# Two picks side by side: a pair of expert rows per visit of the value matmuls, with four PSUM banks

## The chip, the cores and the metric

The kernel runs on one core of a Trainium2 chip. The metric is the device time of one execution in microseconds; for the kernel before there are three runs and one profiled execution.

## What is computed

One layer of a hybrid decoder, in fp32, for a prompt of 1024 positions and 8 sequences of 4 new positions (1056 rows in all): an RMS norm and one input projection feed a convolution, an RWKV head group and stick-breaking attention; their outputs are mixed through one output projection. Then comes the part that the change touches, a product-key mixture of experts (PEER). For each row and each of 8 heads, 16 of 16384 experts are chosen; each expert is one row of a table u and one of a table v:

```python
q = (xb @ w_query).reshape(T, PEER_HEADS, 2, PEER_DK // 2)
s = jnp.einsum('thcd,hcnd->thcn', q, sub_keys)
s1, i1 = lax.top_k(s[:, :, 0], 16); s2, i2 = lax.top_k(s[:, :, 1], 16)
# the 16 x 16 sums, their 16 best (top_s) and the expert numbers e
gate = jax.nn.softmax(top_s, axis=-1)
act = jax.nn.gelu(jnp.einsum('thkd,td->thk', u_tab[e], xb))
return jnp.einsum('thk,thkd->td', (gate * act), v_tab[e])
```

The result is added to the row, and a last RMS norm gives the output.

## The kernel before

The first stages (`project`, `scan_rwkv`, `finish_rwkv`) end at about 990 us. All the rest is `peer`. It works on blocks of 128 rows (`NBLK` = 9, the last one with the 32 sample rows only) and on turns, one head of one block each (`PH` = 8 turns a block). A turn of a full block has 16 picks: for pick k, POOL gathers for each of the 128 rows its k-th expert, u and v rows together, 8 KB a row, into one of 8 slots of `uv` (`RING` = 8). In the last block the 32 rows share the 128 partitions in four groups, so a turn has 4 picks. Picks are taken in pairs (`GP` = 2), numbered m over the whole run.

The engines follow fixed orders written out by hand, with semaphores between them. For each pair:

- POOL (L1270) waits for `uv_free` to reach m - 7 and for the experts of the turn, and issues one gather for each pick.
- DVE (L1535) forms the dot product of u and the normed row, one pick at a time; in between it chooses the experts of the turn after the next (`choose`, L1293 to L1320) in four pieces, and `weigh` (L1342) multiplies gate and activation.
- ACT (L1686) computes the gelu, and (L1694) writes for each pick a diagonal matrix of the weights, `diag`, with a ring of four; each raises `diag_done` by one.
- PE (L1896; L1892 in the last block) multiplies the diagonal with the v half of the slot and accumulates into PSUM over all 128 picks of the block, then raises `uv_free`. It also makes the scores of a later turn (`score`, L1713) and, beside each pair, a piece of attention or output projection for the next block (`beside`).

When a block is complete, DVE adds PSUM to the residual rows `x1` (`add_values`, L1356, L1353). It does so in the next block after that block's first pair has been weighed; PE's first value matmul of the new block waits for it (`summed`). The 64 x 64 matmuls use a quarter of the array each: row half r of the partitions goes to bank `Y[r]`, and the column half j holds columns j*512 to j*512+511 of the output.

In an earlier stage of `peer`, 16 query blocks are folded with the keys into `wk`, with four PSUM banks in rotation (`WK`, L1081).

Of the kernel before, what the change touches and what calls it, by code (L numbers as in the profile page):

```python
# [11 lines left out]
ALU = mybir.AluOpType  # L12
# [4 lines left out]
D = 1024  # L17
# [3 lines left out]
NS = DB * DS  # L21
# [24 lines left out]
PH = 8  # L46
# [923 lines left out]
def peer(nc, io, sb):  # L970

    RING = 8
    GP = 2
# [9 lines left out]
    last = lambda b: b == NBLK - 1  # L983
# [4 lines left out]
    groups_of = lambda t: picks_of(t // PH) // GP  # L988
    after = lambda t: at_pick(t, picks_of(t // PH))
    rows = [slice(r * HT, (r + 1) * HT) for r in range(2)]  # L990
    SUMS = lambda b: 2 if last(b) else 4

    Z, LOGIT, SOFT, LATER, DIFF, OUT, KEEP = 0, 9, 10, 10, 12, 12, 21
    K_PAGES, V_PAGES = -4, 5
# [52 lines left out]
    with ExitStack() as ctx:  # L1047
# [3 lines left out]
        uv = t_("uv_rows", [P, RING, 2 * D])  # L1051
        h2, h2t, x1 = t_("p_h2", [P, 2, D]), t_("p_h2t", [P, DC, P]), t_("p_x1", [P, 2, D])
# [11 lines left out]
        diag = t_("diag", [P, 2 * GP, P])  # L1064
# [11 lines left out]
        zb, sa, sw = logit[:, 0, 0:NK * HQ], logit[:, 1, 0:NK * HQ], soft[:, 0, 0:NK * HQ]  # L1076
        suf = after_[:, :, :].rearrange("p h q -> p (h q)")[:, 0:NPG * HQ]
        ps = lambda name: ctx.enter_context(nc.psum_tensor(name, [P, 512], F32))
        Y = [ps(f"peer_y{r}") for r in range(2)]
        S, B = ps("peer_s"), [ps(f"beside{n}") for n in range(3)]  # L1080
        WK = [Y[0], Y[1], ps("wk_a"), ps("wk_b")]  # L1081
        const_in, close_in, key_in, wq_in = sem("p_const"), sem("p_close_in"), sem("p_key_in"), [sem(f"p_wq_in{n}") for n in range(2)]
        wk_done, wk_kept, eps_set = sem("wk_done"), sem("wk_kept"), sem("p_eps_set")
        uv_in = [sem(f"uv_in{n}") for n in range(RING)]
        dotted, uv_free = sem("dotted"), sem("uv_free")
        gelu_done, weights_done, diag_done = sem("gelu_done"), sem("weights_done"), sem("diag_done")
        score_done, score_kept, exps_done = sem("score_done"), sem("score_kept"), sem("exps_done")
        summed, y_ready, y_out = sem("p_summed"), sem("y_ready"), sem("y_out")
# [188 lines left out]
        def _(dve):  # L1277
# [67 lines left out]
            def add_values(b):  # L1345

                s = b % 2
                dve.wait_ge(uv_free, after(PH * b + PH - 1))
                dve.wait_ge(KV.sem, KV.at("x1", b))
                for k in range(2):  # L1350
                    half = slice(k * 512, (k + 1) * 512)
                    if last(b):
                        nc.vector.tensor_tensor(x1[0:NS, s, half], x1[0:NS, s, half], Y[k][0:NS, :], ALU.add).then_inc(summed, 1)  # L1353
                    else:
                        for r in range(2):
                            nc.vector.tensor_tensor(x1[rows[r], s, half], x1[rows[r], s, half], Y[r][rows[k], :], ALU.add).then_inc(summed, 1)  # L1356

            def normalise(b):

# [164 lines left out]
            for t in range(TURNS):  # L1524
                b, h = divmod(t, PH)
                if h == 0:
                    dve.wait_ge(KV.sem, KV.at("h2", b))
                for q in range(groups_of(t)):
                    g = at_group(t, q)
                    for k in range(GP):  # L1530
                        m = g * GP + k
# [16 lines left out]
                    if not last(b):  # L1548
                        beside(b, h * groups_of(t) + q)
            add_values(NBLK - 1)  # L1550
            normalise(NBLK - 1)

        @block.scalar
        def _(act):
# [9 lines left out]

            def norm(b):
                s, n = b % 2, rows_of(b)
                act.wait_ge(summed, 4 * b + SUMS(b))
                F.did(nc.scalar.activation(h2[0:n, b % 2, :], x1[0:n, s, :], ACT.Square, accum_out=ssq[0:n, 0:1]), "ssq")
                act.wait_ge(F.sem, F.at("ssq", b))
                F.did(nc.scalar.activation(rstd[0:n, :], ssq[0:n, 0:1], ACT.Sqrt, bias=sb.eps[0:n, 0:1], scale=1.0 / D), "root")  # L1570

            def close_root(b):

                act.wait_ge(KV.sem, KV.at("x1", b))
                KA.did(nc.scalar.activation(h2[:, b % 2, :], x1[:, b % 2, :], ACT.Square, accum_out=cssq[:, 0:1]), "ssq")
                act.wait_ge(KA.sem, KA.at("ssq", b))
                KA.did(nc.scalar.activation(crstd[:, :], cssq[:, 0:1], ACT.Sqrt, bias=sb.eps[:, 0:1], scale=1.0 / D), "root")
# [87 lines left out]
            for hc in range(2 * PH):  # L1665
                for j in range(2):
                    act.wait_ge(wk_done, 2 * hc + j + 1)
                    nc.scalar.activation(wk[:, 4 * j:4 * j + 4, hc * P:(hc + 1) * P], WK[(2 * hc + j) % 4][:, :], ACT.Copy).then_inc(wk_kept, 1)
            close_root(0)
# [7 lines left out]
            for t in range(TURNS):  # L1677
                b, h = divmod(t, PH)
                eye = ident4 if last(b) else ident
                n = rows_of(b)  # L1680
                for q in range(groups_of(t)):
# [8 lines left out]
                    for k in range(GP):  # L1690
                        m = g * GP + k
# [13 lines left out]
        def _(pe):  # L1705
            def score(t):
                b, h = divmod(t, PH)
                if h == 0:
                    pe.wait_ge(KA.sem, KA.at("t1", b))
                if t:  # L1710
                    pe.wait_ge(score_kept, t)
                for c in range(DC):
                    ins = nc.tensor.matmul(S[:, 0:HN], h2t[:, c, :], wk[:, c, h * HN:(h + 1) * HN],  # L1713
                                           start=c == 0, stop=c == DC - 1)
                ins.then_inc(score_done, 1)
# [135 lines left out]
            def beside(b, n):  # L1851

                beats(b, n, attend, sample)
                if n - CLOSE in range(DC):
                    close_y(b + 1, n - CLOSE)
                if n == TURN:
                    close_turn(b + 1)
# [5 lines left out]
            for hc in range(2 * PH):  # L1863
                g = hc // WQ
                pe.wait_ge(wq_in[g % 2], 16 * (g // 2 + 1))
                for j in range(2):
                    if hc >= 2:
                        pe.wait_ge(wk_kept, 2 * hc + j - 3)
                    for c in range(4):
                        ins = nc.tensor.matmul(WK[(2 * hc + j) % 4][:, c * P:(c + 1) * P], wq[g % 2][:, hc % WQ, (4 * j + c) * P:(4 * j + c + 1) * P],  # L1870
                                               keys[:, hc, :], start=True, stop=True)
# [9 lines left out]
            for t in range(TURNS):  # L1881
                b, h = divmod(t, PH)
                if h == 0 and b:
                    pe.wait_ge(summed, 4 * b)
                for q in range(groups_of(t)):
                    for k in range(GP):
                        m = at_group(t, q) * GP + k
                        begin, end = h == 0 and q == 0 and k == 0, h == PH - 1 and m + 1 == after(t)
                        pe.wait_ge(diag_done, m + 1)
                        if last(b):  # L1890
                            for j in range(2):
                                ins = nc.tensor.matmul(Y[j][0:NS, :], diag[:, m % (2 * GP), 0:NS],  # L1892
                                                       uv[:, m % RING, D + j * 512:D + (j + 1) * 512], start=begin, stop=end)
                        else:
                            for r, j in ((0, 0), (1, 0), (0, 1), (1, 1)):
                                ins = nc.tensor.matmul(Y[r][rows[j], :], diag[rows[r], m % (2 * GP), rows[r]],  # L1896
                                                       uv[rows[r], m % RING, D + j * 512:D + (j + 1) * 512], start=begin, stop=end)
                        ins.then_inc(uv_free, 1)
                    if q == (1 if groups_of(t) > 1 else 0) and t + LEAD + 1 < TURNS:
                        score(t + LEAD + 1)  # L1900
                    if not last(b):
                        beside(b, h * groups_of(t) + q)
# [158 lines left out]
```

## Time and profile before

| | |
|---|---|
| three runs | 4021.95, 4023.74, 4036.12 us (median 4023.74) |
| the profiled execution | 4021.95 us, of which its span is 4020.1 us |
| PE busy | 2858.3 us, 71% |
| DVE busy | 2654.0 us, 66% |
| ACT busy | 1485.8 us, 37% |
| POOL busy | 1368.1 us, 34% |
| moved by the transfers | 1248.22 MB, mean 310 GB/s |
| mean granted TensorE clock | 0.85 of full speed |

Busy time is summed over the whole span. The span begins with the first instruction and ends with the last; the profiled execution has 1.85 us outside it. An engine that is busy two thirds of the whole may be the limit in one stage and wait in another, so the stages are read one at a time. The DMA share is that of the core's 16 DMA engines, as a mean; it can come out slightly over 1.

### The profile page before, as it was taken

To read this page: it belongs to the slowest core of one execution; us is meant where nothing else is said; L and a number is where in the kernel's file an instruction comes from. 1 tells how busy PE (TensorE), PEld (TensorE's weight loads), DVE (VectorE), ACT (ScalarE), POOL (GpSimd) and SP (SyncE) were. 2 spreads that over 40 slices of the span, in tenths; PEclk is the share of its full clock that TensorE was granted. 3 is DMA by queue.
4 is the path that set the end of the run, shared out by engine and by line. 5 is a ranking of instruction groups with operands and counts; after the bars stand their busy time and mean duration, and the time that the engine had idled before them with its cause. 6 is when DMAs were issued, how large, how long until landed. Compare 5 with 4: busy or idle time off the path is not lost.

```text
span 4020.1 us, 53279 instructions
## 1 busy us (share of the span) xinstructions
PE 2858.3 (71%) x18798; PEld 1340.5 (33%) x18798; DVE 2654.0 (66%) x6645; ACT 1485.8 (37%) x3026; POOL 1368.1 (34%) x1230
## 2 busy tenths in 40 slices
PE   6999777736666676667767676777777766767656
PEld 3545566615222232223223232332323322232211
DVE  1376233342877777877877787678768776777776
ACT  1121222113426234532743483267338522332222
POOL 0000000000443544454354435334444545453421
PEclk8999999868888778878878887888789887788778
DMA  2101100015999999999999999999999999999964
GB/s 81 40 27 59 59 1 0 2 63 181 411 417 408 417 412 411 411 413 415 404 406 414 410 385 417 417 405 404 417 411 405 390 418 413 412 416 411 406 261 169
DMA packets 225745, 1248.22 MB, mean 310 GB/s; under 512 B 33200, under 2 KB 62032, under 8 KB 90224
## 3 DMA queue, kind: packets, MB, share of 16 engines
q0 software_dynamic: 160256, 1132.54, 69.1%
q1 hardware_dynamic: 65264, 112.87, 7.9%
q8 instruction: 118, 1.93, 0.2%
q14 instruction: 107, 0.88, 0.1%
HBM read 1232.20 MB, written 13.11 MB: 310 GB/s over the span
## 4 chain that ended last, share of the span: by engine, by line
DMA 34%; DVE 15%; PE 13%; ACT 7%; issue 5%; POOL 4%; SPq 0%; DVEq 0%; ACTq 0%; POOLq 0%
DMA uv_rows<-in_peer_uv,expert 28%; PE peer_y L1896 8%; DVE uv_rows L1535 5%; DMA pages_ring<-out_k_new 5%; POOL uv_rows L1270 3%; PE peer_s L1713 2%; ACT L1686 1%; ACT diag L1694 1%; ACT L1632 1%; PE peer_y L1892 1%; DVE same L1316 1%; DVE same L1314 1%; DVE pick L1318 1%; DVE weights L1342 1%; PE beside L1734 1%
## 5 line engine op out<-in xcount | busy, mean ns | idle before, releaser
L1896 PE MATMUL peer_y<-uv_rows,diag 64*64 64x512 f32 x8192 | 1285.7, 758 | 793.6 <-ACT diag L1694 772.7
L1270 POOL DMA_INDIRECT uv_rows<-in_peer_uv,expert x1056 | 1201.3, 1138 | 1712.4 <-PE peer_y L1896 1316.2
L1535 DVE CUSTOM_DVE_ANT_0 uv_rows<-uv_rows,p_h 128x1024 f32<-128x1024 f32 x1056 | 1276.5, 1225 | 512.7 <-DMA uv_rows<-in_peer_uv,expert 508.7
L1896 PEld LDWEIGHTS peer_y<-uv_rows,diag 64*64 64x64 f32 x8192 | 318.8, 160 | 1489.0 <-ACT diag L1694 1106.9
L1694 ACT ACTIVATE diag<-p_ident,weights 128x128 f32<-128x128 f32 x1024 | 355.2, 394 | 498.7 <-DVE weights L1342 496.3
L1686 ACT ACTIVATE gelu<-hidden 128x2 f32<-128x2 f32 x528 | 107.4, 203 | 1120.2 <-DVE hidden L1535 1116.1
L523 PE MATMUL proj<-mix,w_in_tile 128*128 128x512 f32 x672 | 298.0, 602 | 18.3 <-DVE mix L332 18.3
L1713 PE MATMUL peer_s<-wk,p_h2t 128*128 128x256 f32 x1152 | 280.1, 398 | 2.3 <-ACT p_h2t L1585 1.3
L1713 PEld LDWEIGHTS peer_s<-wk,p_h2t 128*128 128x128 f32 x1152 | 222.2, 198 | 107.6 <-issue 76.7
L1686 ACT ACT_TABLE_LOAD x196 | 251.5, 1283 | 3.5
L633 POOL COPY v_c<-prc 128x192 f32 (+1 forms) x17 | 5.8, 343 | 627.4 <-POOLq L86 347.5
L523 PEld LDWEIGHTS proj<-mix,w_in_tile 128*128 128x128 f32 x672 | 127.8, 193 | 172.2 <-issue 153.3
L1342 DVE TENSOR_TENSOR weights<-gelu,p_gate 128x2 f32<-128x2 f32 x528 | 85.1, 161 | 130.5 <-ACT gelu L1686 121.2
L1809 PE MATMUL beside<-q_padded,pages_ring 128*128 128x256 f32 x216 | 70.6, 448 | 81.4 <-DMA pages_ring<-out_k_new 80.6
L1892 PE MATMUL peer_y<-uv_rows,diag 128*32 128x512 f32 x128 | 80.9, 796 | 58.8 <-ACT diag L1694 52.8
L1734 PE MATMUL beside<-w_out_rows,mix_block 128*128 128x512 f32 x180 | 93.4, 645 | 22.6 <-DMA w_out_rows<-in_w_out 22.6
L348 DVE TENSOR_TENSOR prc<-prc 128x1088 f32<-128x1088 f32 x11 | 14.2, 1291 | 119.8 <-ACT prc L217 119.8
L1563 ACT ACT_TABLE_LOAD x71 | 91.1, 1283 | 1.3
L212 ACT ACTIVATE prc<-proj 128x512 f32<-128x512 f32 x15 | 9.0, 598 | 221.4 <-PE proj_tails L523 221.4
L1535 DVE DVE_READ_ACCUMULATOR2_ANT hidden<- 128x1 f32 x1056 | 87.5, 83 | 0.0
L1250 POOL DMA_INDIRECT pages_ring<-in_cache_k,page_rows x64 | 76.7, 1199 | 23.0 <-issue 18.9
L1809 PEld LDWEIGHTS beside<-q_padded,pages_ring 128*128 128x128 f32 x216 | 39.8, 208 | 133.1 <-issue 110.5
(324 smaller groups left out, 3935.6 us busy)
## 6 DMA issues: line engine op xcount, KB each, us to landing
w_out_rows<-in_w_out SPq DMA_DIRECT2D x72, 512.0 KB, 8.1
uv_rows<-in_peer_uv,expert POOLq DMA_INDIRECT x1056, 12.5
w_in_tile<-in_w_in SPq DMA_DIRECT2D x24, 512.0 KB, 3.8
uv_rows<-in_w_query SPq DMA_DIRECT2D x4, 2048.0 KB, 10.1
pages_ring<-out_k_new SPq DMA_DIRECT2D x36, 192.0 KB, 31.7
pages_ring<-out_v_new SPq DMA_DIRECT2D x36, 192.0 KB, 25.8
p_x<-in_x_rows SPq DMA_DIRECT2D x9, 512.0 KB, 8.0
mix<-in_xT SPq DMA_DIRECT2D x8, 528.0 KB, 6.8
```

The source lines that it names most:

```text
L523: last = nc.tensor.matmul(out, w[:, i % 3, c, :], h[:, c, lo:lo + size], start=c == 0, stop=c == DC - 1)
L1270: pool.indirect_dma_start(out=uv[:, m % RING, :], out_offset=None, in_=io["peer_uv"], in_offset=bass.IndirectOffsetOnAxis(ap=expert[:, t % ...
L1342: nc.vector.tensor_tensor(wgt[:, g % 2, :], gel[:, g % 2, :], gate[:, t % 4, q * GP:(q + 1) * GP], ALU.mult)\
L1535: nc.vector.tensor_tensor_reduce(out=uv[:, m % RING, 0:D], in0=uv[:, m % RING, 0:D], in1=h2[:, b % 2, :], scale=1.0, scalar=0.0, op0=ALU.m ...
L1563: nc.scalar.activation(expo[:, :], top[:, :], ACT.Exp, bias=neg[:, 0:1], accum_out=esum[:, 0:1]).then_inc(exps_done, 1)
L1686: nc.scalar.activation(gel[:, g % 2, :], hid[:, g % 2, :], ACT.Gelu_apprx_tanh).then_inc(gelu_done, 1)
L1694: nc.scalar.activation(diag[:, m % (2 * GP), 0:n], eye[:, 0:n], ACT.Copy, scale=wgt[:, g % 2, k:k + 1])\
L1713: ins = nc.tensor.matmul(S[:, 0:HN], h2t[:, c, :], wk[:, c, h * HN:(h + 1) * HN], start=c == 0, stop=c == DC - 1)
L1734: ins = nc.tensor.matmul(B[n][:, :], left[:, :], wo[:, c % 2, n * 512:(n + 1) * 512], start=c == 0, stop=c == DC - 1)
L1809: ins = nc.tensor.matmul(B[0][:, i * P:(i + 2) * P], page[:, kt % 4, h // 2 * P:(h // 2 + 1) * P], qpad[:, h:h + 2, :], start=True, stop=True)
L1892: ins = nc.tensor.matmul(Y[j][0:NS, :], diag[:, m % (2 * GP), 0:NS], uv[:, m % RING, D + j * 512:D + (j + 1) * 512], start=begin, stop=end)
L1896: ins = nc.tensor.matmul(Y[r][rows[j], :], diag[rows[r], m % (2 * GP), rows[r]], uv[rows[r], m % RING, D + j * 512:D + (j + 1) * 512], sta ...
```

## The change

The value matmuls visit the picks in pairs. PE waits for both diagonals of a pair (`diag_done` at m + 2), then makes the eight matmuls of a full block with the column half c of the array given to pick m + c, and the two halves of the columns one after the other, each in a bank of its own. So there are four banks, `Y[r][j]`, and partitions 0 to 63 of each hold the sum over the even picks, 64 to 127 that over the odd picks. `uv_free` is raised by 2 after the last matmul of the pair. In the last block the order of the matmuls stays, with the wait and the raise by pairs.

`add_values` now has eight adds for a full block in place of four: those of the even picks first, and after a wait on them those of the odd picks. The counts of `summed` change with that. The two banks `wk_a` and `wk_b` go, and `WK` rotates over the four banks of `Y`.

```diff
--- before.py
+++ after.py
@@ -988,7 +988,7 @@
     groups_of = lambda t: picks_of(t // PH) // GP
     after = lambda t: at_pick(t, picks_of(t // PH))
     rows = [slice(r * HT, (r + 1) * HT) for r in range(2)]
-    SUMS = lambda b: 2 if last(b) else 4
+    SUMS = lambda b: 2 if last(b) else 8
 
     Z, LOGIT, SOFT, LATER, DIFF, OUT, KEEP = 0, 9, 10, 10, 12, 12, 21
     K_PAGES, V_PAGES = -4, 5
@@ -1076,9 +1076,9 @@
         zb, sa, sw = logit[:, 0, 0:NK * HQ], logit[:, 1, 0:NK * HQ], soft[:, 0, 0:NK * HQ]
         suf = after_[:, :, :].rearrange("p h q -> p (h q)")[:, 0:NPG * HQ]
         ps = lambda name: ctx.enter_context(nc.psum_tensor(name, [P, 512], F32))
-        Y = [ps(f"peer_y{r}") for r in range(2)]
+        Y = [[ps(f"peer_y{r}{n}") for n in range(2)] for r in range(2)]
         S, B = ps("peer_s"), [ps(f"beside{n}") for n in range(3)]
-        WK = [Y[0], Y[1], ps("wk_a"), ps("wk_b")]
+        WK = [Y[0][0], Y[0][1], Y[1][0], Y[1][1]]
         const_in, close_in, key_in, wq_in = sem("p_const"), sem("p_close_in"), sem("p_key_in"), [sem(f"p_wq_in{n}") for n in range(2)]
         wk_done, wk_kept, eps_set = sem("wk_done"), sem("wk_kept"), sem("p_eps_set")
         uv_in = [sem(f"uv_in{n}") for n in range(RING)]
@@ -1347,13 +1347,15 @@
                 s = b % 2
                 dve.wait_ge(uv_free, after(PH * b + PH - 1))
                 dve.wait_ge(KV.sem, KV.at("x1", b))
-                for k in range(2):
-                    half = slice(k * 512, (k + 1) * 512)
-                    if last(b):
-                        nc.vector.tensor_tensor(x1[0:NS, s, half], x1[0:NS, s, half], Y[k][0:NS, :], ALU.add).then_inc(summed, 1)
-                    else:
-                        for r in range(2):
-                            nc.vector.tensor_tensor(x1[rows[r], s, half], x1[rows[r], s, half], Y[r][rows[k], :], ALU.add).then_inc(summed, 1)
+                for c in range(1 if last(b) else 2):
+                    if c:
+                        dve.wait_ge(summed, 8 * b + 4)
+                    for r in range(1 if last(b) else 2):
+                        at = slice(0, NS) if last(b) else rows[r]
+                        of = slice(0, NS) if last(b) else rows[c]
+                        for k in range(2):
+                            half = slice(k * 512, (k + 1) * 512)
+                            nc.vector.tensor_tensor(x1[at, s, half], x1[at, s, half], Y[r][k][of, :], ALU.add).then_inc(summed, 1)
 
             def normalise(b):
 
@@ -1564,7 +1566,7 @@
 
             def norm(b):
                 s, n = b % 2, rows_of(b)
-                act.wait_ge(summed, 4 * b + SUMS(b))
+                act.wait_ge(summed, 8 * b + SUMS(b))
                 F.did(nc.scalar.activation(h2[0:n, b % 2, :], x1[0:n, s, :], ACT.Square, accum_out=ssq[0:n, 0:1]), "ssq")
                 act.wait_ge(F.sem, F.at("ssq", b))
                 F.did(nc.scalar.activation(rstd[0:n, :], ssq[0:n, 0:1], ACT.Sqrt, bias=sb.eps[0:n, 0:1], scale=1.0 / D), "root")
@@ -1881,21 +1883,25 @@
             for t in range(TURNS):
                 b, h = divmod(t, PH)
                 if h == 0 and b:
-                    pe.wait_ge(summed, 4 * b)
+                    pe.wait_ge(summed, 8 * b)
                 for q in range(groups_of(t)):
-                    for k in range(GP):
+                    for k in range(0, GP, 2):
                         m = at_group(t, q) * GP + k
-                        begin, end = h == 0 and q == 0 and k == 0, h == PH - 1 and m + 1 == after(t)
-                        pe.wait_ge(diag_done, m + 1)
+                        begin, end = h == 0 and q == 0 and k == 0, h == PH - 1 and m + 2 == after(t)
+                        pe.wait_ge(diag_done, m + 2)
                         if last(b):
+                            for c in range(2):
+                                for j in range(2):
+                                    ins = nc.tensor.matmul(Y[0][j][0:NS, :], diag[:, (m + c) % (2 * GP), 0:NS],
+                                                           uv[:, (m + c) % RING, D + j * 512:D + (j + 1) * 512],
+                                                           start=begin and c == 0, stop=end and c == 1)
+                        else:
                             for j in range(2):
-                                ins = nc.tensor.matmul(Y[j][0:NS, :], diag[:, m % (2 * GP), 0:NS],
-                                                       uv[:, m % RING, D + j * 512:D + (j + 1) * 512], start=begin, stop=end)
-                        else:
-                            for r, j in ((0, 0), (1, 0), (0, 1), (1, 1)):
-                                ins = nc.tensor.matmul(Y[r][rows[j], :], diag[rows[r], m % (2 * GP), rows[r]],
-                                                       uv[rows[r], m % RING, D + j * 512:D + (j + 1) * 512], start=begin, stop=end)
-                        ins.then_inc(uv_free, 1)
+                                for c, r in ((0, 0), (0, 1), (1, 0), (1, 1)):
+                                    ins = nc.tensor.matmul(Y[r][j][rows[c], :], diag[rows[r], (m + c) % (2 * GP), rows[r]],
+                                                           uv[rows[r], (m + c) % RING, D + j * 512:D + (j + 1) * 512],
+                                                           start=begin, stop=end)
+                        ins.then_inc(uv_free, 2)
                     if q == (1 if groups_of(t) > 1 else 0) and t + LEAD + 1 < TURNS:
                         score(t + LEAD + 1)
                     if not last(b):
```

## Rows read from the trace of the kernel before

**Rows 1.** The page: busy time of the engines; the DMA share in 40 slices, in tenths.

```profile
PE 2858.3 (71%) x18798; PEld 1340.5 (33%) x18798; DVE 2654.0 (66%) x6645; ACT 1485.8 (37%) x3026; POOL 1368.1 (34%) x1230
...
DMA  2101100015999999999999999999999999999964
```

**Rows 2.** Window: busy us (x instructions) of PE, PEld, DVE, ACT, POOL; PEclk, DMA share, GB/s.

```profile
1010.00:3850.00 2840.00, 1980.72 (x11262) 804.28 (x11254) 2130.87 (x5513) 1234.26 (x2489) 1312.83 (x1148) 0.83 1.01 410
```

**Rows 3.** Groups of instructions by line: busy us, mean ns, idle before, releasers.

```profile
L1896 PE MATMUL peer_y<-uv_rows,diag 64*64 64x512 f32 x8192 | 1285.7, 758 | 793.6 <-ACT diag L1694 772.7 <-DVE p_x L1356 19.3
L1270 POOL DMA_INDIRECT uv_rows<-in_peer_uv,expert x1056 | 1201.3, 1138 | 1712.4 <-PE peer_y L1896 1316.2 <-issue 154.6 <-DVE best L1293 105.3
L1694 ACT ACTIVATE diag<-p_ident,weights 128x128 f32<-128x128 f32 x1024 | 355.2, 394 | 498.7 <-DVE weights L1342 496.3 <-PE peer_y L1896 2.4
...
L1694 ACT ACTIVATE diag<-ident_groups,weights 128x32 f32<-128x32 f32 x32 | 8.5, 314 | 43.0 <-DVE weights L1342 43.0
```

**Rows 4.** DMA issues of the page: the gathers, median us from issue to landing.

```profile
uv_rows<-in_peer_uv,expert POOLq DMA_INDIRECT x1056, 12.5
```

**Rows 5.** Timeline, one pair at full clock: start us, us, engine, line.

```profile
2399.36 0.69 ACT L1694 ACTIVATE diag<-p_ident,weights 128x128 f32<-128x128 f32 x2 [1.72 <-DVE weights L1342]
...
2400.07 1.95 PE L1896 MATMUL peer_y<-uv_rows,diag 64*64 64x512 f32 x16
```

**Rows 6.** Timeline at the first block boundary.

```profile
1347.34 3.53 PE L1896 MATMUL peer_y<-uv_rows,diag 64*64 64x512 f32 x16 [4.97 <-ACT diag L1694]
...
1350.94 2.84 DVE L1356 TENSOR_TENSOR p_x<-p_x,peer_y 64x512 f32<-64x512 f32 x4 [1.30 <-PE peer_y L1896]
1351.18 0.93 POOL L1270 DMA_INDIRECT uv_rows<-in_peer_uv,expert  x1 [0.62 <-PE peer_y L1896]
...
1353.83 3.60 PE L1896 MATMUL peer_y<-uv_rows,diag 64*64 64x512 f32 x16 [2.97 <-DVE p_x L1356]
...
1356.01 0.98 POOL L1270 DMA_INDIRECT uv_rows<-in_peer_uv,expert  x1 [2.65 <-PE peer_y L1896]
...
1363.49 1.23 DVE L1535 CUSTOM_DVE_ANT_0 uv_rows<-uv_rows,p_h 128x1024 f32<-128x1024 f32 x1 [1.24 <-DMA uv_rows<-in_peer_uv,expert]
```

**Rows 7.** Windows of 4 us behind three block boundaries.

```profile
1711.00:1715.00 4.00, 2.93 (x16) 0.55 (x12) 3.83 (x12) 0.90 (x3) 1.87 (x2) 0.50 1.02 419
...
3153.00:3157.00 4.00, 1.79 (x20) 0.57 (x12) 3.80 (x14) 0.64 (x3) 2.75 (x3) 1.00 0.90 322
...
3865.00:3869.00 4.00, 1.76 (x3) 0.18 (x1) 3.66 (x12) 0.40 (x2) 0.00 (x0) 0.85 0.00 0
```

**Rows 8.** Windows of 10 us: four of the 17 with a share of 0.98 or less.

```profile
1050.00:1060.00 10.00, 10.00 (x63) 3.32 (x56) 9.25 (x25) 5.95 (x11) 5.24 (x5) 0.82 0.98 351
...
2400.00:2410.00 10.00, 6.81 (x69) 2.46 (x68) 9.16 (x23) 4.83 (x10) 6.45 (x6) 0.94 0.82 311
...
3440.00:3450.00 10.00, 6.83 (x58) 3.26 (x50) 6.76 (x20) 1.10 (x4) 7.32 (x6) 0.99 0.93 346
...
3770.00:3780.00 10.00, 8.31 (x52) 3.16 (x45) 7.04 (x21) 1.83 (x7) 6.70 (x6) 0.80 0.98 380
```

**Rows 9.** Timeline of the last block.

```profile
3870.12 1.92 POOL L1270 DMA_INDIRECT uv_rows<-in_peer_uv,expert  x1 [14.39 <-DVE expert L1320]
...
3920.16 0.53 ACT L1694 ACTIVATE diag<-ident_groups,weights 128x32 f32<-128x32 f32 x2 [4.40 <-DVE weights L1342]
...
3920.54 5.32 PE L1892 MATMUL peer_y<-uv_rows,diag 128*32 128x512 f32 x8 [4.62 <-ACT diag L1694]
...
3925.78 3.72 PE L1713 MATMUL peer_s<-wk,p_h2t 128*128 128x256 f32 x16
...
3944.07 5.32 PE L1892 MATMUL peer_y<-uv_rows,diag 128*32 128x512 f32 x8 [4.54 <-ACT diag L1694]
```

**Rows 10.** Timeline of the end: the last two gathers.

```profile
3994.75 0.94 POOL L1270 DMA_INDIRECT uv_rows<-in_peer_uv,expert  x1 [0.31 <-PE peer_y L1892]
...
3997.20 0.94 POOL L1270 DMA_INDIRECT uv_rows<-in_peer_uv,expert  x1 [1.51 <-PE peer_y L1892]
```

## The prediction

> **What bounds the kernel now.** I read the page first, then one row over the long middle of the run, then the line groups, then the timeline at a block boundary and in the last block. The kernel spends its time, from about 1010 us on, in the expert stage: 1056 gathers of 128 rows of 8 KB. The reader should see in the slices of the page that the DMA share stands at nine tenths or more from slice 11 to slice 38, while no compute engine does so over the whole run [rows 1]. The one row over 1010 to 3850 us makes this exact: DMA share 1.01, 410 GB/s; DVE busy 2131 of 2840 us (75%), PE 1981 (70%), POOL 1313 (46%) [rows 2]. A gather of 1.05 MB at 410 GB/s is 2.56 us, and 1024 of them with the rest of the bytes make the stage. So this stage goes at the pace of the transfers, and DVE, the next one, has a quarter of its time free.
>
> The line groups say how this looks from the engines. PE's value matmuls (L1896) waited 794 us, nearly all for ACT's diagonals; POOL waited 1316 us for PE to free a slot before it could issue [rows 3]. The large wait of POOL looks like a bottleneck and is not one by itself: the median gather lands 12.5 us after its issue [rows 4], which at 2.56 us each is 4.9 gathers in flight out of a ring of 8. The engines are behind a queue that is nearly always full. A release of a slot that comes somewhat later takes from these 4.9, not from the transfer rate, until the queue runs dry.
>
> It runs dry in two places. In the middle, the share falls to 0.98 or less in 17 of the 284 windows of 10 us, in 13 separate stretches; the first, the deepest, one with idle engines and the last stand in [rows 8]. Added up, their shortfall against 1.01 is 10 us. And in the last block (from about 3857 us, 4 gathers a turn in place of 16) the transfers are not the limit at all: DMA share 0.00 in a window of four microseconds, right after the boundary [rows 7]. There the time is a chain of DVE, ACT and PE, 23.5 us from one turn's second pair to the next's [rows 9].
>
> **The change, part by part.**
>
> *The matmuls.* Before and after a pair of picks makes 8 matmuls of 64 x 64 over 512 columns in the same order of array quarters (row half 0, then 1; column half 0, then 0, 1, 1), each row half with a bank of its own. 
>
> *The wait for two diagonals.* ACT makes a pair's two diagonals in 0.69 us [rows 5], one in 0.39 by the mean [rows 3]; so PE starts a pair 0.30 us later. Since both uv slots are now released behind the eighth matmul, the first slot of a pair comes free 0.30 + 0.98 = 1.28 us later warm, 0.30 + 1.77 = 2.07 us cold; the second 0.30 us later. Queued behind PE's wait are the scores and the attention of the beat; they are 0.30 us late as well. POOL, which waits for the slots, is next, then the transfer queue. POOL issues at best every 0.94 + 0.30 = 1.24 us, so of two slots freed together the second issue is 1.24 us behind. With 4.9 gathers in flight a delay of 1.3 us costs nothing where the share is 1.01. If that cover were gone each of the 512 pairs would pay 1.28 us, 655 us in all; it is gone only where the queue is dry.
>
> The Trainium skill (DMA: Bandwidth & Descriptors, Anatomy of one DMA) gives a gather a fixed cost of about 2.0 us plus bytes at 436 GB/s, so 4.4 us for one of these as an estimate from that page. By it two gathers in flight keep the queues fed, the 4.9 could fall by three before anything is lost, and the term for the dry stretches below would be nearer 0; no row here shows one gather alone.
>
> *The dry stretches in the middle.* In nine of the 13, DVE or ACT is busy 90% or more of a window: there a slot that comes later is made up, since the engine and not the gather is late. In four (1480, 3440, 3630, 3770 us) no engine is that busy, as in the row at 3440 us with DVE at 68% and ACT at 11% [rows 8]. There the release sets when transfers resume. I take 4 x 1.28 = 5.1 us; from below 0, from above all 13 cold, 27 us.
>
> *The adds.* add_values makes 8 adds of 64 x 512 at a full block's end in place of 4. Four take 2.84 us [rows 6], so four more are 2.84 us of DVE; the wait of the second four on the first costs no more than DVE's usual step, as the adds are done in order. This comes 8 times. PE waits for it before the first value matmul of the block (2.97 us idle already [rows 6]), and with it the first slots: POOL's gap from 1351.18 to 1356.01 us grows from 4.8 to about 4.8 + 2.84 + 1.28 to 2.07, so 9 to 10 us. The gather issued before the gap is used at 1363.5 us at the earliest, 12.3 us after its issue [rows 6], so even the long gap is just covered. At 6 of the 7 boundaries of the middle the share is 0.99 or more around the adds, as in the row at 1711 us; I cost these at 0, from above 6 x (2.84 + 2.07) = 29 us. At the one near 3149 us it is 0.90 [rows 7], no cover there: 2.84 + 1.28 = 4.1 us.
>
> *The last block.* Here the share of 0.00 stands at 3865 us [rows 7]. At the boundary (3857 us) DVE makes the adds ahead of the choice that gives POOL its next experts, and POOL sat 14.39 us for those [rows 9]; 2.84 us in full. Each turn runs through PE's second pair (5.32 us), then the scores (3.72 us) to ACT and DVE; PE's start waits for ACT [rows 9]. Two diagonals of 32 columns take 0.53 us [rows 9] against 0.31 for one by the mean of 32 [rows 3], so 0.22 us later in each of 5 turns that still make scores, and once before the end: 6 x 0.22 = 1.3 us. At the end the last two gathers are issued at 3994.75 and 3997.20 us, each as its slot comes free [rows 10]; after, both wait for the second release, and the last is issued 0.22 + 1.24 = 1.5 us later. This one is on the chain that ended last (DMA 9.2 us behind that issue).
>
> *Banks and semaphores.* Two more banks for Y, the same two fewer for wk: eight before and after, and the rotation of four in the wk stage is the same. 0 us.
>
> **Sum:** 2.84 + 1.3 + 1.5 + 4.1 + 5.1 = 14.9 us. Against the profiled execution's own 4021.95 us (span 4020.1 and 1.9 around it) this gives 4037. The median of the three runs lies 1.8 us higher, so I say **4039 us**. A measurement of this kernel tells about 0.5% (20 us) from no change, so this counts as no change, on the slow side.
>
> **Rivals.**
>
> *The ring runs dry (slower).* Pairwise release and the longer gap at boundaries take from one reserve. If the reserve is thinner than the median says, windows that now stand at 0.99 to 1.00 turn into dry ones. It decides when a gather in flight lands before the next issue has got through, that is, when POOL's gap passes the 12.3 us less what a gather needs. For it: the stretch at 2400 us stands at 0.82 [rows 8], so the reserve does run out under load. Against it: 267 of 284 windows are full. Price: all bounds together, 2.84 + 1.3 + 1.5 + 27 + 7 x 4.9 = 67 us, so 4091; half-way 4060.
>
> *All of the middle is absorbed.* Only the last block pays: 5.6 us, 4029 us. For it: DMA share 1.01 on average; even the dry stretches are mostly DVE's and ACT's.
>
> *Fewer, better grouped gathers move faster (faster).* A full window such as that at 1711 us moves 419 GB/s [rows 7], the middle 410 [rows 2]. If gathers issued in twos mixed less with the page loads between them, half of that 2.2% over 2840 us would come back, 31 us, with 5.6 lost: 3998. Against it: the bytes and the page loads stay, and a share of 1.01 leaves no idle time to win. PE passes that overlap better could not do it, since only 10 us of dry queue are there to be had.
>
> **Chances.** Forecast (8 to 20 us slower) 0.37; absorbed (within 8 us of before, or slightly less) 0.21; ring dry (over 20 us slower) 0.34; faster 0.08. Hence faster by over 0.5%: 0.07, within 0.5%: 0.58, slower by over 0.5%: 0.35. The range holds 8 in 10: at the low end it leaves out most of the faster case, 4018; at the high end the top third of the way to all bounds, 4080.
>
> **What the profile after would show.** The adds: 64 records at line L1356's successor in place of 32, of 0.69 us, 5.7 us a boundary. PE: value matmuls unchanged in number and mean, 16 passes in 1.95 us warm. POOL: issues in twos 1.24 us apart, its wait for PE larger. Gathers: fewer in flight, so 0.5 to 1.5 us less than 12.5 from issue to landing. Middle: share 1.01 still, each block as long as now. The last block 5 to 6 us longer. I am wrong if the blocks of the middle grow by over 3 us each, if windows at a share under 0.98 are more than about 25, or if the passes of a pair take another time than 1.95 us.

## The result

The changed kernel takes 4051.25 us in the median of seven runs (4039.76 to 4056.88), the kernel before 4029.19 (4021.95 to 4036.48). The ratio is 1.0053, with a 95% interval of 1.0037 to 1.0069: slower by about 21 us (15 to 28 by the interval), where 15 were forecast.

The two profiled executions lie further apart, 4020.1 and 4053.4 us of span. So I first looked for places that are the same in both and compared from there. The first value matmul starts at 1008.7 us before and at 1020.5 us after, and the code up to there does the same work; 10 of these 12 us arise in the scan stage (its matmuls in L761 run from 476.9 to 771.4 us before, from 478.0 to 782.7 after). That is another execution, not the change: over the profiles of this kernel and of the ten of the experiments the first value matmul starts anywhere from 1009.5 to 1029.2 us. From the first value matmul to the end it is 3011.4 us before and 3032.9 after: 21.5 us, which agrees with the timed runs. From here on I call this stretch the expert stage and compare it.

The page after: busy time, and the share of the transfers.

```profile
PE 2863.6 (71%) x18798; PEld 1350.9 (33%) x18798; DVE 2671.7 (66%) x6677; ACT 1485.9 (37%) x3026; POOL 1364.3 (34%) x1230
...
DMA  2101100015999999999999999999999999999964
...
uv_rows<-in_peer_uv,expert POOLq DMA_INDIRECT x1056, 11.4
```

Against [rows 1] and [rows 4]: DVE has 32 more instructions and 17.7 us more work; a gather now lands 11.4 us after its issue where it took 12.5. The two medians are not of the same gathers: the traces tell the landing of 401 of the 1056 before and of 797 after. Over the 401 that both have it is 12.5 and 11.3 us, so the fall holds. At the middle's rates 11.4 us is 4.4 gathers in flight in place of 4.9: the reserve is smaller. The middle window and the groups by line:

```profile
1010.00:3850.00 2840.00, 1963.13 (x11202) 801.63 (x11202) 2138.72 (x5516) 1231.48 (x2480) 1305.49 (x1147) 0.83 1.00 408
```

```profile
L1901 PE MATMUL peer_y<-uv_rows,diag 64*64 64x512 f32 x8192 | 1275.8, 753 | 814.4 <-ACT diag L1696 778.0 <-DVE p_x L1358 35.0
L1270 POOL DMA_INDIRECT uv_rows<-in_peer_uv,expert x1056 | 1210.5, 1146 | 1735.7 <-PE peer_y L1901 1280.0
...
L1358 DVE TENSOR_TENSOR p_x<-p_x,peer_y 64x512 f32<-64x512 f32 x64 | 41.2, 683 | 10.5 <-PE peer_y L1901 9.7
```

The value matmuls are as many and as long as in [rows 3] (753 ns in the mean against 758), so four banks changed nothing in the time of PE's passes. POOL's idle time before its gathers grew from 1712 to 1736 us, but the part that the page puts down to PE fell, from 1316 to 1280. The share of the transfers went from 1.01 to 1.00 and the rate from 410 to 408 GB/s [rows 2]. Such small steps in a mean are the whole loss of the middle: in windows of 10 us from 1030 to 3850 us there were 17 with a share of 0.98 or less (dry windows, for short), with 10.2 us missing to 1.01; now there are 21, with 25.6 us missing. The two deepest, with DVE busy 98% in the one and ACT 97% in the other, and two behind a boundary:

```profile
1060.00:1070.00 10.00, 9.51 (x56) 3.11 (x60) 9.79 (x25) 5.97 (x13) 4.19 (x3) 0.75 0.75 285
1280.00:1290.00 10.00, 7.79 (x36) 2.24 (x36) 8.83 (x24) 9.66 (x17) 2.81 (x2) 0.66 0.75 283
...
2090.00:2100.00 10.00, 8.64 (x44) 3.82 (x37) 9.39 (x30) 2.69 (x9) 5.63 (x6) 0.71 0.83 319
...
3180.00:3190.00 10.00, 9.09 (x68) 4.46 (x60) 8.51 (x26) 5.19 (x10) 5.58 (x5) 0.93 0.76 279
```

Before, the lowest window was at 0.82 [rows 8]. The first block boundary after the change, in the timeline, with the same steps as [rows 6]:

```profile
1365.76 5.25 DVE L1358 TENSOR_TENSOR p_x<-p_x,peer_y 64x512 f32<-64x512 f32 x8 [1.65 <-PE peer_y L1901]
...
1367.23 0.93 POOL L1270 DMA_INDIRECT uv_rows<-in_peer_uv,expert  x1 [0.30 <-issue]
...
1371.06 3.69 PE L1901 MATMUL peer_y<-uv_rows,diag 64*64 64x512 f32 x16 [5.38 <-DVE p_x L1358]
...
1375.06 0.94 POOL L1270 DMA_INDIRECT uv_rows<-in_peer_uv,expert  x1 [5.64 <-PE peer_y L1901]
1376.30 1.03 POOL L1270 DMA_INDIRECT uv_rows<-in_peer_uv,expert  x1 [0.30 <-issue]
```

Eight adds take 5.25 us, PE stands 5.38 us for them, and only when its eight matmuls are through are two slots free at once; POOL issues the two gathers 1.24 us apart. Between gather and gather lie 7.8 us (1367.23 to 1375.06) in place of 4.8. Then the transfers fall short, in windows of 4 us:

```profile
1370.00:1374.00 4.00, 2.94 (x16) 0.80 (x16) 3.93 (x9) 0.20 (x1) 0.00 (x0) 0.50 1.01 410
1374.00:1378.00 4.00, 2.64 (x16) 0.68 (x16) 3.59 (x12) 0.90 (x3) 2.33 (x3) 0.50 0.88 309
```

Last, the last block. It takes 171.8 us from its adds to the end in place of 162.8. The last two gathers and the last pair of PE:

```profile
4025.61 0.94 POOL L1270 DMA_INDIRECT uv_rows<-in_peer_uv,expert  x1 [2.97 <-PE peer_y L1895]
4026.85 1.26 POOL L1270 DMA_INDIRECT uv_rows<-in_peer_uv,expert  x1 [0.30 <-issue]
...
4038.84 6.61 PE L1895 MATMUL peer_y<-uv_rows,diag 128*32 128x512 f32 x8 [3.21 <-ACT diag L1696]
```

As in [rows 10], but both now wait for the same release. The last pair took 6.61 us, where the kernel before needed 3.62. Of the 9.0 us, 2.6 arise from the adds to the first turn's second pair, 1.5 in the next five turns, 1.9 on the way from there to the last pair, and 3.0 in that pair.

### The profile page after: what moved, and what is told of

Its sections match the earlier page's. It is cut to its first block, busy times and chain, and to the rows that moved or that the text cites. A ratio compares the mean times of both kernels' runs of the same rounds, so it can differ in the third digit from the quotient of the medians.

```text
span 4053.4 us, 53311 instructions
## 1 busy us (share of the span) xinstructions
PE 2863.6 (71%) x18798; PEld 1350.9 (33%) x18798; DVE 2671.7 (66%) x6677; ACT 1485.9 (37%) x3026; POOL 1364.3 (34%) x1230
## 4 chain that ended last, share of the span: by engine, by line
DMA 30%; DVE 16%; PE 14%; ACT 7%; issue 5%; POOL 4%; SPq 0%; DVEq 0%; ACTq 0%; POOLq 0%
DMA uv_rows<-in_peer_uv,expert 24%; PE peer_y L1901 9%; DVE uv_rows L1537 5%; DMA pages_ring<-out_k_new 5%; POOL uv_rows L1270 4%; PE peer_s L1715 2%; ACT L1688 2%; ACT diag L1696 2%; DMA w_out_rows<-in_w_out 1%; ACT L1634 1%; PE beside L1736 1%; DVE p_x L1358 1%; PE peer_y L1895 1%; DVE same L1316 1%; DVE same L1314 1%
## 5 line engine op out<-in xcount | busy, mean ns | idle before, releaser
L1823 PE MATMUL beside<-soft,s_tri 128*128 128x512 f32 (+1 forms) x112 | 75.2, 760 | 8.1 <-DVE soft L1470 8.0
## 6 DMA issues: line engine op xcount, KB each, us to landing
uv_rows<-in_peer_uv,expert POOLq DMA_INDIRECT x1056, 11.4
```

## The experiments

Two parts of the change could be at fault, with a different remedy each: the pairing (a wait for two diagonals, a release of two slots) and the double adds. A third possibility is the form of the matmuls itself; no run has it alone. The first four kernels take the kernel before and do one part alone; the next four start from either kernel and turn one size or one part; the last two follow from what the last block showed. Ratios are to the kernel before, timed on the same chip in the same rounds. Beside them stands the expert stage of the profile, in two parts: from the first value matmul to the adds of the last block (the middle, seven boundaries) and from there to the end (the last block).

| kernel | ratio, 95% interval | middle, us | last block, us |
|---|---|---|---|
| before | 1 | 2848.6 | 162.8 |
| after | 1.0053 [1.0037, 1.0069] | 2861.1 | 171.8 |
| e1 pair only | 1.0018 [1.0005, 1.0032] | 2857.2 | 167.0 |
| e2 adds only | 1.0017 [1.0003, 1.0030] | 2852.9 | 167.2 |
| e3 wait only | 1.0003 [0.9988, 1.0019] | 2847.7 | 162.5 |
| e4 release only | 1.0020 [1.0007, 1.0033] | 2854.7 | 163.0 |
| e5 before, ring of 6 | 1.0452 [1.0421, 1.0483] | 3033.3 | 165.5 |
| e6 after, ring of 6 | 1.0886 [1.0860, 1.0912] | 3196.5 | 171.9 |
| e7 after, last block by pick | 1.0035 [1.0023, 1.0046] | 2861.0 | 166.4 |
| e8 after, split wait | 1.0042 [1.0028, 1.0056] | 2861.5 | 167.4 |
| e9 before, scores early | 0.9921 [0.9905, 0.9938] | 2850.9 | 128.3 |
| e10 after, scores early | 0.9956 [0.9938, 0.9973] | 2861.4 | 135.3 |

How far to trust one profile's middle: the same middle was profiled four times in after's form (after, e7, e10, and e8 but for the wait) with 2861.0 to 2861.5 us, and twice in before's form with 2848.6 and 2850.9. So I read differences of over 3 us in this column. It is a judgement from few profiles: the 4.3 us of e2 become 2.0 against e9. The last block scatters more, because PE's clock falls differently in it: e8 has the same code there as the kernel after and took 167.4 us, not 171.8.

**e1, the pairing alone.**

```diff
-                        pe.wait_ge(diag_done, m + 1)
+                        if k == 0:
+                            pe.wait_ge(diag_done, m + GP)
...
-                        ins.then_inc(uv_free, 1)
+                        if k == GP - 1:
+                            ins.then_inc(uv_free, GP)
```

> The kernel before with the wait for both diagonals and the release of both slots together, and nothing else: no further banks, four adds. Theory (late release and adds share the cost): from the first value matmul to the end of the span about 10 to 13 us more than before, of which about 3 in the last block and the rest spread over the blocks; in total time 0.2 to 0.35% slower. Rival (the eight adds at each boundary are all of it, 8 x 2.4 us): no more than 3 us, same time within 0.1%. Rival (form of the matmuls, four banks): also no more than 3 us.

Measured: 1.0018, the expert stage 12.8 us longer, 4.2 of it in the last block. It came out as the first theory had it. Of the six windows at 0.89 or less, five (1070 us: 0.73, 2050: 0.85, 2360: 0.83, 2420: 0.89, 2720: 0.87) do not lie at boundaries (the row after 1370 and that after 2090 us stand at 1.02 and 1.01); the sixth (3190: 0.88) is behind the boundary at which the kernel before falls short as well [rows 7]. PE is busy 99% or more in those five; DVE or ACT is busy 90% in three of them, and in those at 2050 and 2420 us neither is over 71%.

**e2, the adds alone.** The four adds made twice, with the wait between; the output holds the value sums twice.

```diff
+                for c in range(1 if last(b) else 2):
+                    if c:
+                        dve.wait_ge(summed, 8 * b + 4)
                     for k in range(2):
```

> The kernel before with the four adds of each full block made twice, the second four behind a wait on the first; the value sums are so added twice, which the output shows. Theory: about 8 to 10 us more than before behind the first value matmul: 2.6 at the last boundary, the rest where a boundary meets a dry queue; 0.2% slower. Rival (adds are all of it): 19 to 22 us, 0.5% slower, each block 2.4 us longer. Rival (form of the matmuls): at most 3 us.

Measured: 1.0017, the expert stage 8.7 us longer: 4.4 in the last block, 4.3 in the middle over seven boundaries, not 2.4 at each. The rival that made the adds the whole cause falls. Here the new dry windows do lie just behind boundaries (1710 us: 0.85, 2070: 0.85, 2790: 0.92, 3150: 0.81).

The dry windows tell the two parts of the change apart. I added up what is missing to 1.01 in them, at boundaries (a window that starts from 5 us before the adds to 20 us behind them) and elsewhere: before 1.7 and 8.5 us, e1 1.7 and 17.8, e2 10.7 and 5.5, after 8.2 and 17.4. The pairing costs away from the boundaries, the adds cost at them, and the changed kernel has both.

By the profiles 12.8 and 8.7 make 21.5, which is the distance of the changed kernel and would leave nothing for the form of the matmuls. The timed runs are less sure: 0.18% and 0.17% against 0.53% leave 0.18%, 7 us, with intervals of 0.13 to 0.16% on each of the three. So a cost of the form of some us is not excluded by them; against it speaks that PE's passes took the same time.

**e3 and e4, the halves of the pairing.** e3 has only the first edit of e1, e4 only the second.

> The kernel before with PE waiting for both diagonals before the first pick of a pair, slots still released one by one. Theory: the start is only 0.30 us later (0.22 in the last block), so 2 to 3 us in all, same time within 0.1%. Rival (the wait is what costs, since PE's scores and attention stand behind it): as much as the pair kernel, 10 us or more.

> The kernel before with each pick started on its own diagonal but both slots of a pair released behind the second. Theory: this is the costly half of the pairing, 7 to 10 us behind the first value matmul, with the middle's dry windows up from 17 towards 21; 0.2% slower. Rival (the wait is the costly half): no more than 3 us.

Measured: the wait alone 1.0003, the expert stage 1.2 us shorter, which is no difference (2 to 3 us were expected); the release alone 1.0020, 6.3 us longer, a little under the 7 to 10 expected, with 25 dry windows. By the middles, 2847.7 and 2854.7 us, the late release is the costly half; the timed ratios point the same way, but their intervals overlap. By the profiles the halves do not add up to the pair (5 us against 12.8), by the timed runs they do (0.03% and 0.20% against 0.18%); with intervals of 0.13% to either side I can't say whether they work on each other.

**e5 and e6, a ring of 6 slots.** One line, `RING = 6`, in the kernel before and in the changed one.

> The kernel before with a ring of 6 slots in place of 8. It is the base of the next run. Theory (a reserve of gathers in flight hides the processing): the reserve falls by two, dry windows become many, 2 to 6% slower. Rival (the queue is full anyway, 2 gathers in flight suffice): within 0.5%.

> The changed kernel with a ring of 6 slots. Theory (pairwise release spends the reserve): its distance to the kernel before with the same ring grows from 21 us to 60 us or more behind the first value matmul, since nearly each of the 512 pairs now pays part of its 1.28 us. Rival (the pairing costs a fixed amount at boundaries, in the last block and in the few stretches that DVE and ACT make dry): the distance stays near 21 us.

The middle windows of the two, e5 and then e6:

```profile
1030.00:3850.00 2820.00, 1911.22 (x10586) 767.27 (x10578) 1999.64 (x5140) 1178.99 (x2348) 1235.24 (x1078) 0.81 0.98 385
```

```profile
1030.00:3850.00 2820.00, 1853.83 (x10042) 741.33 (x10038) 1922.88 (x4911) 1138.82 (x2246) 1147.01 (x1019) 0.80 0.94 365
```

Measured: 4221.75 and 4398.18 us. With two slots fewer the same change costs 176 us in place of 22, and in the profiles the expert stage is 3198.8 and 3368.4 us long, 0.33 us a pair apart. DVE and PE are less busy in both than in [rows 2], so no engine has taken over; the transfers are what fell, to shares of 0.98 and 0.94 and to 385 and 365 GB/s, while the gathers landed 9.0 and 8.3 us after their issue. This is the strongest evidence for the reserve: nothing in the pairing's own work depends on the size of the ring. Adds and pairing were not run apart with six slots.

**e7, the changed kernel with the last block by pick.**

```diff
                         if last(b):
                             for c in range(2):
+                                pe.wait_ge(diag_done, m + c + 1)
                                 for j in range(2):
...
+                                ins.then_inc(uv_free, 1)
```

> The changed kernel with the last block as before: wait and release pick by pick. Theory: the last block gets back 0.22 us a turn and the 1.2 us at the last gather, with the clock that the later last pair lost 4 to 5 us together; 3028 us from the first value matmul to the end in place of 3032.9. Rival (the last block's loss is the adds' alone): within 1 us of the changed kernel there.

Measured: the last block 166.4 us, 5.4 less than after; the expert stage 3027.4 us. The number is as expected, but it doesn't decide: e8 below, whose last block has the code of the kernel after, took 167.4 us there, and the timed medians of the two are 4052.58 and 4052.69 us. So 1.0 us may be all that the edit brought, as much as the rival had; the rest came with the clock of the last pair.

**e8, the wait of the changed kernel split.**

```diff
                                 for c, r in ((0, 0), (0, 1), (1, 0), (1, 1)):
+                                    if j == 0 and r == 0:
+                                        pe.wait_ge(diag_done, m + c + 1)
```

> The changed kernel with PE waiting for the first diagonal before the first pick's matmuls and for the second only ahead of the second pick's; release in pairs as changed. Theory: gets back the 0.30 us a pair on PE only, at most 3 us in all. Rival (wait and release multiply, since pair kernel minus release kernel was 6 us): 5 to 7 us back.

Measured: 1.0042, the expert stage 4.0 us shorter than after, but all of it in the last block, whose code is the same in both; there the last pair came 8.60 us behind the second pair of the turn before and not 10.23, PE had been idle 1.56 us, and the pair ran at the fast clock in 3.62 us. The middle is at 2861.5 us, no gain: with the release at the end of the pair, an earlier start buys nothing. The theory's bound of 3 us holds with nothing to spend it on; the rival's 5 to 7 us are not there.

**e9 and e10, the scores of the last block earlier.** In the last block DVE sat idle 33.4 us in five turns before L1293 until the scores were copied, and the scores stood behind PE's second pair [rows 9]. The edit puts them behind the first pair; full blocks are as they were.

```diff
-                    if q == (1 if groups_of(t) > 1 else 0) and t + LEAD + 1 < TURNS:
+                    if q == (1 if groups_of(t) > 2 else 0) and t + LEAD + 1 < TURNS:
```

> The kernel before, where in the last block PE makes the scores of a later turn behind the first pair of a turn and not behind the second. In the last block DVE idles 6.2 to 6.4 us a turn until those scores are copied; they stand behind a PE pair of 5.3 us. Theory (the last block is a chain of DVE, ACT and PE and not of transfers): 5 turns lose most of this wait, 20 to 30 us less than before, 0.5 to 0.7% faster. Rival (the transfers of the last block come next, since 4 gathers of 2.6 us and their landing stand in each turn): less than 10 us.

> The changed kernel with the same move of the scores in the last block. Theory: the same gain, and the distance of about 21 us to the kernel before with that move stays, less the 1.1 us of the turns (5 x 0.22), as PE's second pair no longer stands in the chain of a turn. Rival (pairwise release becomes costly once a turn is shorter): distance 30 us or more.

POOL in e9 in one turn of the last block, to be read against the 23.5 us a turn of [rows 9]:

```profile
3944.61 1.92 POOL L1270 DMA_INDIRECT uv_rows<-in_peer_uv,expert  x1 [11.57 <-DVE expert L1320]
3946.83 0.94 POOL L1270 DMA_INDIRECT uv_rows<-in_peer_uv,expert  x1 [0.30 <-issue]
3948.07 0.94 POOL L1270 DMA_INDIRECT uv_rows<-in_peer_uv,expert  x1 [0.30 <-issue]
3949.32 0.93 POOL L1270 DMA_INDIRECT uv_rows<-in_peer_uv,expert  x1 [0.31 <-issue]
3961.81 1.92 POOL L1270 DMA_INDIRECT uv_rows<-in_peer_uv,expert  x1 [11.56 <-DVE expert L1320]
```

A turn is 17.2 us (3944.61 to 3961.81), and DVE no longer waits before L1293. e9 takes 4008.57 us in the median, 0.79% less than the kernel before and faster than both; in the profile the last block fell by 34.5 us, more than I expected. In e10 the change still costs 17.5 us against e9 by the profiles (10.5 in the middle, 7.0 in the last block) and 13.4 by the timed medians, less than the 20 of the theory and far from the rival's 30.

## Why the prediction was nearly right

The forecast was 4039 us and 14.9 us of cost; measured are 4051.25 us and 21.5 us in the expert stage. Of the 12 us between the two times, about 5 come from its starting point: the median before was 4023.74 us of three runs and is 4029.19 of seven. By its own branches the cost lies just over the edge of the one it thought likeliest (8 to 20 us, 0.37), in the one of the dry ring (over 20 us, 0.34). Point by point, by the terms of the sum:

*The matmuls, 0 us: right for their time.* 16 passes in 1.95 us warm, as forecast: the row at 3087.40 us below, against [rows 5].

```profile
3087.40 1.95 PE L1901 MATMUL peer_y<-uv_rows,diag 64*64 64x512 f32 x16 [0.30 <-ACT diag L1696]
```

*The limit and the mechanism: right.* The middle goes at the pace of the transfers, the change spends a reserve of gathers in flight, and it costs where the reserve is out. The landing time fell by 1.1 us, inside the 0.5 to 1.5 that I had named. The runs with six slots show it. The number of dry windows is not as firm: 21 in this profile, but 28 to 31 in the three others of the changed form (e7, e8, e10). My sign of being wrong was more than about 25 under 0.98; by that count it is 19 here and 23 to 25 in the three, so it was nearly reached. What is missing in the dry windows, 24.5 to 26.0 us, agrees in all four, and so do the middles.

*The middle, 9.2 us forecast, 12.5 measured: a size, from two steps.* For boundaries I had 4.1 us, at one of seven, and wrote of the others that "even the long gap is just covered". It is not: of the six, those at 1722, 2083 and 3531 us are followed by windows of 0.90, 0.83 and 0.92. The gap itself was 7.8 us, less than the 9 to 10 of my sum, and still transfers were missed behind it; so comparing it with the 12.3 us from issue to use of a gather was the wrong test. As I read it, that test treats a queue with one gather left in it as one that still runs full; no run measures this by itself. For the dry stretches I had 5.1 us; the pairing by itself cost 8.6 in the middle (e1). I had set the stretches in which DVE or ACT is 90% busy to nothing (by the trace there are 14 stretches, ten of them such, not 13 and nine). But the deepest windows of the changed kernel are such ones: 0.75 at 1060 and at 1280 us, where the kernel before stands at 0.97 or more from 1040 to 1080 and from 1260 to 1290 us. That an engine is busy 90% in a window did not make up for a gather that came late in it. I had also looked at DVE and ACT only, and not at PE, which releases the slots and was busy 99% or more in five of e1's six deepest windows.

The rule of the Trainium skill would have moved the sum the wrong way. By the 4.4 us for a gather, an estimate from it (DMA: Bandwidth & Descriptors, Anatomy of one DMA), two in flight keep the queues fed; here, with 3.3 in flight by the medians of the six-slot ring (9.0 us to landing, 2.7 us each at 385 GB/s), 6% of the rate was gone. No run has one gather alone, so the page's figure itself is not tested. A median says how much is in flight on the whole and not how much is left at the end of a gap.

*The adds, 2.84 us: 2.41.* Eight take 5.25 us where I had scaled four to 5.68.

*The last block, 5.6 us forecast, 9.0 measured: a size.* The adds with 2.4 and the turns with 0.22 us were right: a turn is 23.75 us where it was 23.5 (3996.27 to 4020.02 us, from second pair to second pair; turns with PE on the slow clock are up to 1 us longer). The last gather is issued 7.38 us behind the first of its turn where it was 5.92, so 1.5 us later, as forecast. Missing in the sum is the clock: PE had been idle 3.21 us and not 1.30 before the last pair, and took 6.61 us at a granted clock of 0.54, where it had taken 3.62 at 1.00. That is 3.0 us. It doesn't come every time: e8, with the same code in the last block, shows 167.4 us and a fast last pair, 4.6 us more than before, and e6 against e5 shows 6.4, with six slots. Against those two the forecast of 5.6 is good, and part of its error is chance of one execution.

*Rivals.* "The ring runs dry" was the nearer of them in kind, since boundaries and loaded stretches do run dry, but its half-way price of 36 us is not reached with eight slots. "All absorbed" is out, since the middle is 12.5 us longer. For "faster" there is no sign: the rate fell.

Still open is how wait and release of the pairing divide their 12.8 us, and by how much the pairing and the adds work on each other at boundaries; the profiles add up exactly, which with some 2 us of scatter each is in part luck, and the timed runs do not settle it. Nor does any run have the form of the matmuls alone.

## What to carry to other kernels

When a kernel goes at the pace of its transfers, the point at which a buffer is given back is part of the critical resource: the same change cost 0.5% with eight slots and 4% with six, while the engines were less busy. Judge the reserve at the worst gap, not by a median time to landing, and don't cost a late release at nothing just because an engine is busy nearby. And look at the last, thinner block by itself: it was bound by something else than the rest, and moving one group of matmuls there brought 28 us in the timed runs, more than the whole change had cost.

## What the runs showed of the hardware

The clock of TensorE at a late, short burst. The last pair is the same eight passes in each kernel; its row in the pair kernel e1:

```profile
4040.10 5.25 PE L1893 MATMUL peer_y<-uv_rows,diag 128*32 128x512 f32 x8 [2.43 <-ACT diag L1694]
```

and in e10, the changed kernel with the scores early:

```profile
4012.50 5.32 PE L1895 MATMUL peer_y<-uv_rows,diag 128*32 128x512 f32 x8 [2.22 <-ACT diag L1696]
```

Windows over the last pair, of before and then of after (the third value from the end is the granted clock):

```profile
4008.53:4012.16 3.63, 3.62 (x8) 0.80 (x8) 0.00 (x0) 0.16 (x1) 0.00 (x0) 1.00 0.01 2
```

```profile
4038.84:4045.46 6.62, 6.61 (x8) 1.24 (x8) 0.00 (x0) 0.00 (x0) 0.00 (x0) 0.54 0.00 1
```

Where PE had been idle for 0.4 to 1.6 us (six profiles) it ran at 2.4 GHz and took 3.62 us; after 2.43 us of idleness it took 5.25; after 2.22 us (e10) it took 5.32; after 3.21 us it ran nearly all of it at 1.2 GHz and took 6.61. In e1 and e10 the granted clock over the pair was 0.68. So from the kernel before to the changed one, 1.9 us more of idleness ahead of a short burst came with 3.0 us more in the burst.

The same code before the first value matmul took from 1009 to 1029 us in the profiles. In the stretch from 470 to 770 us the granted clock was 0.95 to 0.97 in the three executions that came there at 1008.7 to 1012.8 us, and 0.90 to 0.93 in the nine that came at 1018.7 us or later. A spread of 20 us from there is as large as the effect studied, and is the reason to compare from a common point of the trace.
